# Folding the second accumulator of an MoE kernel into the output between the last jobs instead of after them

## What is computed

```python
x = x + y_mix @ w_out[l]                        # x1: 1024 x 1024, float32
xn = rms_norm(x, ffn_norm_w[l]).reshape(Bsz * S, D)
x = x + moe_ffn(xn, w_router[l], ...)           # out = x1 + routed + shared
# in moe_ffn: each token goes to 8 of 64 experts
y = swiglu(x_pad[tok], w_eg[e], w_eu[e], w_ed[e]) * weight
routed = zeros.at[tok].add(y)
return routed + swiglu(xf, w_sg, w_su, w_sd)
```

## Time and profile before

| | |
|---|---|
| three timed runs | 1725.65, 1726.55, 1728.88 us; median 1726.55 |
| the profiled execution's own time | 1726.42 us |
| its span (first to last instruction) | 1724.7 us |
| mean granted TensorE clock | 0.944 |
| PE busy | 1574.0 us, 91% of the span |
| DVE, POOL, ACT busy | 661.8, 582.9, 293.9 us |

### The profile page before, as it was taken

One profiled execution on the slowest core, in us unless ns is written; L12 is line 12 of the kernel. 1 busy time (PEld: TensorE's weight loads), 2 busy tenths in 40 slices (PEclk: granted clock), 3 DMA queues, 4 the chain that ended last, 5 costly groups with the idle time before them and its releaser, 6 DMA issues.

```text
span 1724.7 us, 24638 instructions
## 1 busy us (share of the span) xinstructions
PE 1574.0 (91%) x6759; PEld 700.1 (41%) x6760; DVE 661.8 (38%) x883; ACT 293.9 (17%) x573; POOL 582.9 (34%) x629
## 2 busy tenths in 40 slices
PE   7789889999996799899999999999999999998890
PEld 3355455455555444333333333333333333333230
DVE  1233343442533333344444444444444444443240
ACT  1223323223223000011111111111111111111010
POOL 2001202212122220145444444545454444444242
PEclk9899999898896799899999999999999999999895
DMA  9101101002033532478889897877889978887625
GB/s 356 72 13 43 43 25 43 37 21 52 17 122 160 115 107 88 165 248 272 306 269 330 266 326 250 267 238 265 247 268 332 334 255 269 276 294 254 222 28 112
DMA packets 71888, 319.37 MB, mean 185 GB/s; under 512 B 14791, under 2 KB 16328, under 8 KB 46388
## 3 DMA queue, kind: packets, MB, share of 16 engines
q1 hardware_dynamic: 41764, 237.52, 37.6%
q0 software_dynamic: 30096, 81.50, 19.5%
HBM read 279.59 MB, written 60.89 MB: 197 GB/s over the span
## 4 chain that ended last, share of the span: by engine, by line
PE 87%; DMA 4%; DVE 3%; issue 2%; POOL 1%; SPq 1%; ACT 1%; DVEq 0%; POOLq 0%; ACTq 0%
PE psP L618 50%; PE psW L618 27%; PE psT L755 5%; PE psW L785 2%; DMA area<-in_x_dram 1%; DMA u_dram<-zrow 1%; PE psW L664 1%; PE psT L624 1%; DVE area L1217 1%; DMA wts<-in_w_exp_gate_dram 1%; PE psT L695 1%; DVE area L1113 1%; ACT area L898 0%; DMA x_dram<-area,sidx 0%; SPq L350 0%
## 5 line engine op out<-in xcount | busy, mean ns | idle before, releaser
L618 PE MATMUL psP<-wts,area 128*64 (+2 forms) x2032 | 899.1, 597 | 38.8 <-issue 19.8
L618 PE MATMUL psP<-area 128*64 128x512 f32 x1264 | 569.2, 604 | 0.0
L618 PEld LDWEIGHTS psP<-wts,area 128*64 128x64 f32 (+1 forms) x2032 | 319.1, 162 | 531.2 <-issue 522.3
L618 PE MATMUL psW<-wts,area 128*64 128x512 f32 (+2 forms) x1592 | 432.6, 599 | 2.3 <-DVE wts L1435 1.5
L579 POOL DMA_INDIRECT out_dram<-area,sidx x79 | 218.8, 2769 | 428.8 <-issue 320.3
L618 PEld LDWEIGHTS psW<-wts,area 128*64 128x64 f32 (+1 forms) x1592 | 143.2, 147 | 218.4 <-issue 217.4
L1428 DVE COPY area<-wts 128x4096 f32 x81 | 185.8, 2294 | 119.8 <-issue 90.7
L1435 DVE COPY wts<-wts 128x2048 f32 x79 | 96.9, 1227 | 187.9 <-PE psW L618 187.9
L618 PEld LDWEIGHTS psP<-area 128*64 128x64 f32 x1264 | 168.9, 139 | 0.0
L1344 DVE SCALAR_TENSOR_TENSOR kv_sb<-kv_sb,area,psP 128x256 f32<-128x256 f32 x79 | 53.1, 673 | 269.3 <-ACT kv_sb L1022 269.3
L1038 ACT ACTIVATE area<-psW 128x1024 f32<-128x1024 f32 x79 | 81.0, 1025 | 341.5 <-PE psW L618 194.3
(11 more groups left out here) (201 smaller groups left out, 834.7 us busy)
## 6 DMA issues: line engine op xcount, KB each, us to landing
wts<-in_w_exp_gate_dram SPq DMA_DIRECT2D x64, 1024.0 KB, 4.8
wts<-in_w_exp_up_dram SPq DMA_DIRECT2D x64, 1024.0 KB, 6.8
wts<-in_w_exp_down_dram SPq DMA_DIRECT2D x64, 1024.0 KB, 10.4
wts<-in_w_in_dram SPq DMA_DIRECT2D x4, 2048.0 KB, 17.6
area<-in_x_dram SPq DMA_DIRECT2D x8, 512.0 KB, 3.3
wts<-in_w_out_dram SPq DMA_DIRECT2D x1, 4096.0 KB, 18.3
area<-u_dram SPq DMA_DIRECT2D x16, 256.0 KB, 3.3
xn_dram<-area POOLq DMA_DIRECT2D x8, 512.0 KB, 3.0
```

The costliest lines, as they stand in the source:

```text
L618: return nc.tensor.matmul(out_, lhsT, rhs, start=start, stop=stop)
```

## The change

Up to the last eight jobs (nine where `n` is odd, as here), nothing changes in what is added where; the loop on GpSimd now has two jobs in its body instead of four. The last jobs are written out one by one. In them

- both blocks are added into `out`, one after the other: the second is issued when the first has landed, and the first when all of the job before has landed;
- `x1_dram` is complete when they begin, so it is merged into `out` in pieces of 128 rows (512 KB), one after each of the first six of these jobs and two after the seventh. A piece is issued when the job's second block has landed, and the next job's first block waits for it (`s_merged`);
- the gather for job r+3 stays ahead of job r's adds, so it now stands behind the piece of job r-1. Two gathers past the last job are dropped.

At the end GpSimd waits for the gathers alone; SP waits for the adds and the pieces. DVE computes two more numbers in the routing stage (L1422 area): `n` less 8, and half of that.

```diff
--- before.py
+++ after.py
@@ -208,7 +208,7 @@
         ringB_i = sb("ringB_i", [P, JT], I32)
         jend_f = bi.bitcast(I32)
         jend_i = sb("jend_i", [P, NE], I32)
-        n_jobs = sb("n_jobs", [P, 10], I32)
+        n_jobs = sb("n_jobs", [P, 12], I32)
         slot_i = sb("slot_i", [P, NT * 8], I32)
         pay = sb("pay", [P, NT, 8, 2])
         tok_i = sb("tok_i", [P, NT, 8], I32)
@@ -301,6 +301,9 @@
         N_SL = 5
         CD = 13
         J_TAB = 3
+        AHEAD = 3
+        LAST = 8
+        PIECES = (1, 1, 1, 1, 1, 1, 2)
 
         def front(eng, step):
 
@@ -444,7 +447,7 @@
             n = sp.value_load(n_jobs[0:1, 0:1], min_val=MIN_JOBS, max_val=JMAX)
             for b in range(2):
                 sp.wait_ge(s_added[b], n * 16)
-            sp.wait_ge(s_merged, 8 * S // P)
+            sp.wait_ge(s_merged, 16 * NT)
             carry(sp)
 
 
@@ -566,20 +569,18 @@
                                         in_offset=bass.IndirectOffsetOnAxis(ap=gidx[:, par:par + 1], axis=0),
                                         bounds_check=S - 1, oob_is_err=False).then_inc(g_ld[par], 16)
 
-            def scatter(j, par, copies):
-
-                nc.gpsimd.tensor_copy(sidx[0][:, par:par + 1], tab_i[0:HB, bass.ds(j - NSH, 1)]).then_inc(s_idx_cp, 1)
-                nc.gpsimd.tensor_copy(sidx[1][:, par:par + 1], tabB_i[:, bass.ds(j - NSH, 1)]).then_inc(s_idx_cp, 1)
+            def copy_idx(r, par, copies):
+                nc.gpsimd.tensor_copy(sidx[0][:, par:par + 1], tab_i[0:HB, bass.ds(r, 1)]).then_inc(s_idx_cp, 1)
+                nc.gpsimd.tensor_copy(sidx[1][:, par:par + 1], tabB_i[:, bass.ds(r, 1)]).then_inc(s_idx_cp, 1)
                 pool.wait_ge(s_idx_cp, copies + 2)
-                pool.wait_ge(s_y_ready, j + 1)
-                for b in range(2):
-                    r = slice(b * HB, (b + 1) * HB)
-                    pool.wait_ge(s_added[b], (j - NSH) * 16)
-                    carry(pool)
-                    pool.indirect_dma_start(out=(out2, x1_dram)[b][:, :],
-                                            out_offset=bass.IndirectOffsetOnAxis(ap=sidx[b][:, par:par + 1], axis=0),
-                                            in_=ysb[r, par], in_offset=None, bounds_check=S - 1,
-                                            oob_is_err=False, compute_op=ALU.add).then_inc(s_added[b], 16)
+                pool.wait_ge(s_y_ready, r + (NSH + 1))
+
+            def add_block(dst, b, par):
+                carry(pool)
+                pool.indirect_dma_start(out=dst[:, :],
+                                        out_offset=bass.IndirectOffsetOnAxis(ap=sidx[b][:, par:par + 1], axis=0),
+                                        in_=ysb[b * HB:(b + 1) * HB, par], in_offset=None, bounds_check=S - 1,
+                                        oob_is_err=False, compute_op=ALU.add).then_inc(s_added[b], 16)
 
             pool.wait_ge(s_tab, 3)
             gather(NSH, 0, 0)
@@ -589,27 +590,46 @@
             for b in range(2):
                 pool.wait_ge(sh_st[b], 8 * NSH)
             pool.wait_ge(s_n_jobs, 4)
-            n = pool.value_load(n_jobs[0:1, 0:1], min_val=MIN_JOBS, max_val=JMAX)
-
-            def jobs(i, ks):
-                for k in ks:
-                    j = i * 2 + (NSH + k)
-                    gather(j + 3, 1 - k, i * 6 + (3 + 3 * k))
-                    scatter(j, k, i * 6 + (4 + 3 * k))
-
-            routed_jobs(pool, 0, jobs)
-
-            pool.wait_ge(g_ld[0], ((n + 4) // 2) * 16)
-            pool.wait_ge(g_ld[1], ((n + 3) // 2) * 16)
+            pairs = pool.value_load(n_jobs[0:1, 11:12], min_val=(MIN_JOBS - LAST) // 2, max_val=(JMAX - LAST) // 2)
+            with pool.Fori(0, pairs) as i:
+                for k in range(2):
+                    r = i * 2 + k
+                    gather(r + (NSH + AHEAD), (k + AHEAD) % 2, i * 6 + (AHEAD + 3 * k))
+                    copy_idx(r, k, i * 6 + (AHEAD + 1 + 3 * k))
+                    for b, dst in ((0, out2), (1, x1_dram)):
+                        pool.wait_ge(s_added[b], r * 16)
+                        add_block(dst, b, k)
+
+
+            def last_job(i, copies):
+                r = pairs * 2 + i
+                if i < LAST - 1:
+                    gather(r + (NSH + AHEAD), (i + AHEAD) % 2, copies)
+                    copies = copies + 1
+                copy_idx(r, i % 2, copies)
+                for b in range(2):
+                    pool.wait_ge(s_added[b], r * 16)
+                if i >= 1:
+                    pool.wait_ge(s_merged, 16 * sum(PIECES[0:i]))
+                add_block(out2, 0, i % 2)
+                pool.wait_ge(s_added[0], r * 16 + 16)
+                add_block(out2, 1, i % 2)
+                if i < LAST - 1:
+                    pool.wait_ge(s_added[1], r * 16 + 16)
+                    carry(pool)
+                    for a in range(sum(PIECES[0:i]), sum(PIECES[0:i + 1])):
+                        pool.dma_start(out2[a * P:(a + 1) * P, :], x1_dram[a * P:(a + 1) * P, :], accum_op=ALU.add,
+                                       max_dma_last_dim=8192).then_inc(s_merged, 16)
+
+            for i in range(LAST):
+                last_job(i, pairs * 6 + (AHEAD + 3 * i))
+            one = pool.alloc_register("one_last")
+            pool.reg_load(one, n_jobs[0:1, 8:9])
+            with pool.If_ne(one, 0):
+                last_job(LAST, pairs * 6 + (AHEAD + 3 * LAST - 1))
+            gathers = AHEAD + LAST - 1
             for b in range(2):
-                pool.wait_ge(s_added[b], n * 16)
-            carry(pool)
-            rows = 2 * P
-            for a in range(S // rows):
-                pool.dma_start(out2[a * rows:(a + 1) * rows, :].rearrange("(p r) n -> p (r n)", r=2),
-                               x1_dram[a * rows:(a + 1) * rows, :].rearrange("(p r) n -> p (r n)", r=2),
-                               accum_op=ALU.add, max_dma_last_dim=8192).then_inc(s_merged, 16)
-            pool.wait_ge(s_merged, 16 * S // rows)
+                pool.wait_ge(g_ld[b], (pairs + (gathers + 1 - b) // 2) * 16)
 
 
         @block.tensor
@@ -1401,6 +1421,10 @@
             dve.wait_ge(s_post, 10)
             V.tensor_scalar(n_jobs[:, 2:4], n_jobs[:, 0:2], 1, None, ALU.arith_shift_right).then_inc(s_n_jobs, 1)
             V.tensor_scalar(n_jobs[:, 4:6], n_jobs[:, 0:2], 2, None, ALU.arith_shift_right).then_inc(s_n_jobs, 1)
+            V.tensor_scalar(n_jobs[:, 10:11], n_jobs[:, 0:1], -float(LAST), None, ALU.add).then_inc(s_post, 1)
+            dve.wait_ge(s_post, 11)
+            V.tensor_scalar(n_jobs[:, 11:12], n_jobs[:, 10:11], 1, None, ALU.arith_shift_right).then_inc(s_post, 1)
+            dve.wait_ge(s_post, 12)
             dve.wait_ge(s_n_jobs, 2)
             V.scalar_tensor_tensor(out=n_jobs[:, 6:8], in0=n_jobs[:, 4:6], scalar=-2.0, in1=n_jobs[:, 2:4],
                                    op0=ALU.mult, op1=ALU.add).then_inc(s_n_jobs, 1)
```

## The result

| | before | after |
|---|---|---|
| timed runs beside each other | 1726.23 us (4: 1725.65 to 1728.88) | 1742.70 us (4: 1741.14 to 1743.28) |
| ratio, 95% interval | | 1.0092 (1.0076 to 1.0108) |
| the profiled execution's own time | 1726.42 us | 1741.14 us |
| its span | 1724.7 us | 1739.3 us |
| last landing | 1718.2 us | 1734.1 us |

The change makes the kernel 16.5 us slower. The page of the changed kernel shows it in the chain that ended last: PE's share falls from 87% to 81%, and that of transfers rises from 4% to 10%. They are the adds (`out_dram<-area,sidx`) and the pieces (`out_dram<-x_dram`).

What follows compares the result with a forecast made beforehand. PE was taken to bound the kernel (87% of the last-ending chain). A 136.9 us GpSimd chain would land last at 1714.8, gaining 3.4 us, plus 1.1 at the close: 1726.42 - 3.4 - 1.1 = 1721.9 us; range 1713 to 1731.

Steps and rivals of the forecast that it cites:

- What bounds the kernel, and what takes its place: PE bounds; 23.2 us between last block and last landing are the prize, bought with a serial chain on GpSimd.
- GpSimd is behind, not ahead: At job 74: its first block starts at 1651.7 instead of 1644.32; then 15 us a job against PE's 12.
- C: Rival, waits between adds: each landing costs more than its half of a pair; 1733 us, 1737 at 5.1 a block; chance 0.17.
- Hand-overs: From a landing to GpSimd's next issue: seven of 0.61 us and seventeen of 0.11, together 5.9 us.
- Blocks: Adds of the last nine jobs, one at a time: seventeen at 4.2 us and a last of 2.5, together 73.9.
- Pieces: Merge pieces between the last jobs: six at 5.0 us and a double one of 7.9, together 37.9.
- Beside weight loads: Chain steps during SP's loads, until some 1633 us: about four steps at 3.0 us extra, together 12 us.
- Beside DVE's copies: GpSimd issues meeting DVE's weight copies: about 0.4 us each on some 18 issues of jobs 70 to 76, 7.2 us.
- PE behind GpSimd: Gathers behind pieces cost PE some 3 us a job, perhaps 10 in all, without costing the kernel anything.
- The close: At the end GpSimd's DRAIN may begin earlier, before the last landing: 1.1 us gained.
- The small parts: Two DVE routing instructions and the shorter loop body: below 0.5 us and some ten nanoseconds a turn, even uncovered.
- B: Rival: GpSimd keeps PE's pace and job 74 starts at 1644.32 as before; 1714.3 us; chance 0.10.

## Where the prediction went wrong, step by step

**What bounds the kernel, and what takes its place.** That the gain lies behind PE's last job, and that a serial chain on GpSimd would set the end, held: see the chain of after, and the kernel with freed gathers. So did "GpSimd is behind, not ahead": job 74's first add came at 1664.34. I had given 1651.7 for it, and 1656 or later for C. By then 12.6 of the 19.3 us were lost.

**Hand-overs: the step that failed.** "A block 0.11 after (1690.61 to 1690.72)" is wrong. That row names `x_dram<-area,sidx` as the releaser, but a first block does not wait for that semaphore. The chain of the kernel before shows what happened. Ahead of job 77's first add its sequencer step (L579) stands at 1681.25 and the add at 1682.00. The step at 1690.71, after the landing at 1690.61, is that of the *second* add. The first add's own step (the move of L579 in GpSimd's sequencer, which is off this chain) stands at 1689.6, a microsecond ahead of that landing, and its start beside the landing is chance.

```profile
1681.25 0.03 POOLq L579
...
1682.00 0.67 POOL out_dram L579
...
1685.50 5.11 DMA x_dram<-area,sidx
...
1690.71 0.03 POOLq L579
1690.74 0.58 POOL out_dram L579
...
1692.49 2.51 DMA x_dram<-area,sidx
```

In the same kernel without its merge the last job's first add is also idle for 1.34 us after its index copies, and there the row names no landing:

```profile
1693.01 1.47 POOL L578 DMA_INDIRECT out_dram<-area,sidx  x1 [1.34 <-issue]
```

The true price was to be had from the same trace: ACT ended its read-out at 1680.98 (1679.96 + 1.02), and the waiting add was issued at 1682.00, 1.02 us later. In the changed kernel the sixteen that can be measured cost 14.3 us, 0.89 each. Seventeen at 0.9 instead of 0.1 are 13.6 us, which alone takes the sum from 1721.9 to 1735.5. So the mechanism, a serial chain on GpSimd, was right, and the term that failed is the hand-overs: 5.9 us forecast, 18.4 measured, 12.5 of the 17.5 us.

**Blocks.** 4.2 was right for the quiet ones (4.24). How I got there was in part luck: I took two in 5.4 us as "about 3" for one, and then less than the 4.5 that came out. **Pieces.** 5.0 was somewhat low: quiet ones took 5.14 to 6.35. The rule of the Trainium skill (DMA: Bandwidth & Descriptors, "Anatomy of one DMA") is 2.0 us plus the bytes at 436 GB/s. An estimate by it is 3.2 us for 512 KB and 2.6 for a full block. The runs disagree for these adding transfers, with 5.14 and 3.40 us at the least (the very last block, 2.56, apart); not to price by it was right.

**Beside weight loads.** Four steps at 3.0 were too few and too cheap: three blocks cost 3.2, 6.3 and 4.4 more, and the piece at 1637.97 some 3 on top. C's doubt ("four to six blocks run beside a load") was nearer in kind, though it was three, and a fourth in the last part of one. That the loads would end at 1633 was also wrong: the last one, late by PE's wait, ran to 1650. **Beside DVE's copies.** The longer issues came as described: 2.24, 2.31 and 3.37 us instead of 1.41 for a second add. The copies also met what I had not counted, gathers (3.19, 2.39, 2.45 instead of 1.08) and a piece (1.92 instead of 0.87). The Trainium skill (SBUF — State Buffer, the box on "DVE blocks DMA") says that GpSimd cannot write the descriptors of its transfers while DVE's copy holds the port that they share. The trace agrees here too: each of these issues overlaps a copy of weights. Blocks, pieces, loads and copies together are 5.0 us over.

**PE behind GpSimd.** It lost 23 us, not 10 (last read-out at 1708.67, before 1685.49). As forecast this set no end: job 77 was added at 1716.08, 12 us after its read-out, and freeing the gathers gained nothing. **The close.** 1.3 us of gain, forecast 1.1. **The small parts** (two DVE instructions, the shorter loop body) show nothing: job 70's first add began between 1577.0 and 1581.0 us in the kernels that have them, and at 1577.85 and 1580.40 in the kernel before, with and without its merge.

**The rivals.** The sign was C's, and the time lies above its 1737. But its price, 5.1 us for every block, was not the cause: the blocks without a load beside them took 4.3 on the mean. The rest was a term that none of the rivals doubted, because all four took the hand-over from the same misread row. The range ended at 1731 for that reason. B is excluded by job 74's first add alone.

## What to carry to other kernels

Price a wait by a place where the waiting engine was ready and the wait ended last, and check the releaser that a trace infers against the semaphores in the code. In these runs a serial chain was nearly free as long as it fitted into the cycle of the engine that covers it, and cost its excess in every turn beyond that: two changes that cost 5.3 and 3.6 us apart cost 37.4 together. The two kernels that beat the one before move the closing work into the pipeline once and whole, with the next gather ahead of it and only five or seven jobs in turn behind it. The one that does it where no load runs has the lower median, 1718.1 against 1720.4 us.

## What the runs showed of the hardware

- In the changed kernel GpSimd needs 0.86 us from the landing that it waits for to the start of an indirect transfer, 0.95 where a job begins, and 0.58 for a plain one.
- Over all runs its closing DRAIN after such transfers takes 5.7 to 8.7 us: 5.75 to 6.08 where it begins at the last landing, 7.1 to 8.7 where it begins before it. I had thought that the merge might make it long, but it took 5.75 without any merge. It ends 4.5 to 6.1 us after the last landing. In the kernel before without its merge:

```profile
L71 POOLq DRAIN  x1: 5746/5746/5746, 1697.4 to 1697.4; - x1
```

- One block of up to 64 rows of 4 KB, added into DRAM, takes 3.4 to 5.4 us without a load beside it in the changed kernel, and 7.4 to 10.5 beside a load of weights for most of its time. The longest of any run is 11.4, in the kernel with turns in all jobs. Where it is not waited for, that is hidden; in turn, it is the time of the kernel.
